# Mixer projections in three fp32r products, with the weights split on ScalarE, VectorE and GpSimd

## The chip, the core and the metric

The kernel runs on one core of one Trainium2 chip, as one program. The metric is the device time of that core in microseconds (us), from the start of the execution to its end. A profile of one execution, taken by the hardware profiler, stands beside the times; its span is the time between its first and its last recorded instruction.

## What is computed

The input `x` is 256 tokens of 1024 numbers in fp32. Four layers follow one another, each of a mixer and a feed-forward part. Cut to what matters:

```python
# first_block: two layers, with a norm behind each part as well
for layer in range(2):
    h = rmsnorm(x, norm_mix_pre[layer])
    m = attention_mixer(h, ...) if layer % 2 == 0 else recurrent_mixer(h, ...)
    x = x + rmsnorm(m, norm_mix_post[layer])
    h = rmsnorm(x, norm_ffn_pre[layer])
    x = x + rmsnorm(swiglu(h, ffn_w_gate[layer], ffn_w_up[layer], ffn_w_down[layer]), norm_ffn_post[layer])
# second_block: two layers
x = x + dilated_diff_mixer(rms_norm(x, attn_norm), ...)
x = x + swiglu_2(rms_norm(x, ffn_norm), ...)
x = x + hgrn2_mixer(rms_norm(x, hgrn_norm), ...)
x = x + moe_swiglu(rms_norm(x, moe_norm), ...)        # 8 experts, top 2, 3584 hidden units

def recurrent_mixer(h, w_in, ...):
    gate, xr = jnp.split(h @ w_in, 2, axis=-1)        # w_in: 1024 x 2048
    gate = jax.nn.gelu(gate, approximate=True)
    xc = causal_conv(xr, conv_w) + conv_b             # four taps
    r = sigmoid(xc @ w_a + b_a); i = sigmoid(xc @ w_i + b_i)   # in four blocks of 256
    ...                                               # a, sqrt(1 - a*a), a scan over the tokens: hs
    return (hs * gate) @ w_out
```

Each mixer begins with `h @ w_in`: its projection. The widths of the four `w_in` are 3072 (attention), 2048 (recurrent), 3072 (dilated and differential attention) and 4096 (HGRN2). These products are what the change rewrites.

## The kernel before, in words

**Stages.** The program has eight stages, in the order of the reference: `A` (attention mixer), `F` 0, `R` (recurrent mixer), `F` 1, `E` (dilated and differential attention), `F` 2, `G` (HGRN2) and `M` (the experts, in a loop over the eight of them). Below, first mixer means `A`, second `R`, third `E`, fourth `G`. Each stage has a function for each engine (`R_tensor`, `R_scalar`, `R_vector`); the order of its statements is the order of the instructions on that engine, and semaphores tie the engines together. Nothing reorders them: an instruction that waits holds up everything behind it on its engine.

**Weights.** SyncE loads all weights in units of 1 MB (128 partitions x 2048 fp32) in one fixed order into a ring of slots, five in the first seven stages and seven in `M`. A slot has the unit as loaded (`slot_raw`) and room for two fp32r parts of it: `slot_hi`, a rounded copy, and `slot_lo`, what the copy leaves over (the weights minus the high part). In the trace these are `ring`, and `ring_r` with the half 1 and 0 in its number. A slot is free for the next load when TensorE has counted `w_used` for its unit.

**Two kinds of product.** The feed-forward parts and the experts split each unit: ScalarE copies it (`highs_to`, a helper that does so for all units up to a given one that are not done yet; it waits for `landed`), VectorE subtracts (`lows_to`), and TensorE makes three fp32r products for each pair: high x high, high weight x low feature, low weight x high feature. The mixers' projections do not: `project` makes their units with `columns_of(w, c0, False)`, `weights_ready` waits for the load alone, and `by_columns` and `by_tokens` do one plain fp32 matmul on `slot_raw` and on the features in fp32 (`HTf`). A unit of a mixer is 256 columns of `w_in` over all 1024 features; by columns ("F" and "X" units) it makes 2 x 8 matmuls of 256 moving columns (the tokens), by tokens ("H" units) as many of 256 moving columns (the weights). The out projections (`project_out`) are plain fp32 in both kernels, and so are the gates of `R` (L1208).

**First units.** `first_tokens` runs the first three or four units of a mixer for tokens 0 to 127 first, in matmuls of 128 columns for "F" and "X" units, then for tokens 128 to 255. `unit_tensor` runs a later unit, `unit_scalar` evacuates it (L576) from PSUM (`ps`) with the function that the stage wants.

**Norms.** Between two stages each token half goes through sums of squares on ScalarE (`post_sums`, `norm_sums`), a small power on GpSimd (`norm_gpsimd`, which counts `s_rstd`), the gain on VectorE (`normalise_tokens`, L422), eight transposes on TensorE (`norm_turn`, L441) and evacuation of these. In front of a feed-forward part the evacuation gives a high part by ScalarE (`norm_high`, L368) and a low part by VectorE (`norm_low`, L433); in front of a mixer (`k % 2 == 0`) ScalarE and VectorE each copy half of it in fp32. There are two orders written out by hand: `norm_scalar` and `norm_vector` for mixers, `ffn_norm_scalar` and `ffn_norm_vector` for feed-forward parts, where copies and low parts of the first weights are interleaved.

**The second mixer's order.** TensorE: units 0 to 3 (the branch with the convolution), the gates of the first half, unit 4, the gates of the second half, units 5, 6, 7, out projection. ScalarE: convolution inputs, sigmoids of gates (L1250), tanh, exp (L1257), square roots (L1261), and only then the evacuations of units 4 to 7 with gelu (L576).

**The third and fourth mixer.** In `E` VectorE has a chain of reciprocals and gains (L1533, L1535) for the normalised queries and keys, and behind it the bias additions to the scores (L1546); ScalarE's squares (L1453) precede it. In `G` L576 evacuates the first units, and functions on ScalarE and VectorE follow before TensorE transposes (L1639).

**Entry to `M`.** ScalarE copies three units (`split_high`, L1953), then does the sums of both token halves; VectorE does the three low parts (`split_low`, L1958), then residual, gain and evacuation of both halves (L413, L422, L2146), then the arithmetic of the router (L2174 is a line of it). An expert gathers its tokens by fp32r matmuls of 128 columns (L1972).

**GpSimd** does the small powers, constants at the start (L795, L796) and issues the loads of the gain rows (`gpre`, `gpost`).

## Time and profile before

| | before |
|---|---|
| three executions, median (lowest to highest) | 2214.52 us (2212.74 to 2216.56) |
| profiled execution, its own time | 2214.71 us |
| span of the profiled execution | 2212.6 us |
| mean granted TensorE clock | 0.989 |
| TensorE busy | 2152.9 us, 10426 matmuls |
| VectorE busy | 1412.0 us |
| ScalarE busy | 1182.0 us |
| GpSimd busy | 42.6 us |

The page names engines PE (TensorE), DVE (VectorE), ACT (ScalarE), POOL (GpSimd) and SP (SyncE). `L509` is line 509 of the kernel; `ps<-arena,ring` names what is written and what is read. Views of the trace are: the page's busy shares; groups of instructions by line, where with shapes apart a group is one line, engine, operation and tile; the chain of work that ended last, followed back from the last instruction and shown in order of time; and the timeline of one engine. Matmuls are pipelined, and one that starts before the previous one ends overlaps it in the records, so that starts of successive matmuls tell what one costs. Idle time in square brackets stands ahead of an instruction with what released it.

### The profile page before, as it was taken

What the parts mean: (1) busy time and instruction counts of PE and PEld (TensorE: products, weight loads), DVE (VectorE), ACT (ScalarE), POOL (GpSimd) and SP (SyncE); (2) the same over time, 40 slices, a digit from 0 to 9 for tenths busy, and PEclk for the clock granted to TensorE, in tenths of its full rate; (3) what the DMA queues carried; (4) which work ended last, traced back from release to release, by engine and by line L of the source; (5) the groups of instructions that cost most, each with busy time, mean ns of one, the idle gap of its engine ahead of it and who ended that gap; (6) DMA issues with size and microseconds to landing.
All of it is one profiled execution on the core that took longest, in us unless ns stands there. A gap on an engine that the chain in (4) does not pass through costs nothing.

```text
span 2212.6 us, 26593 instructions
## 1 busy us (share of the span) xinstructions
PE 2152.9 (97%) x10426; PEld 1755.4 (79%) x10426; DVE 1412.0 (64%) x1193; ACT 1182.0 (53%) x1107; POOL 42.6 (2%) x94
## 2 busy tenths in 40 slices
PE   7999999999999999999996999999999999999998
PEld 7757889868888658889874888888888888888887
DVE  1425444454444635443725888889888988888887
ACT  1335432444423544333533677677766777767775
POOL 1001000010000000000000000000000000000000
PEclk9999999999999999999996999999999999999999
DMA  7325554555554226555423999999999999999997
GB/s 250 115 77 187 191 184 149 183 174 189 189 172 143 96 86 209 184 178 162 134 77 115 359 354 351 376 341 363 348 358 349 362 348 356 372 338 373 342 362 262
DMA packets 208180, 539.60 MB, mean 244 GB/s; under 512 B 10046, under 2 KB 67487, under 8 KB 208111
## 3 DMA queue, kind: packets, MB, share of 16 engines
q1 hardware_dynamic: 204224, 530.61, 67.7%
q0 software_dynamic: 2096, 7.87, 1.0%
q8 instruction: 51, 0.84, 0.2%
q10 hardware_dynamic: 1790, 0.14, 0.1%
q14 instruction: 19, 0.15, 0.0%
HBM read 537.54 MB, written 1.05 MB: 243 GB/s over the span
## 4 chain that ended last, share of the span: by engine, by line
PE 89%; ACT 5%; DVE 2%; issue 2%; DMA 1%; POOL 1%; DVEq 0%; ACTq 0%; POOLq 0%
PE ps L1962 12%; PE ps L1964 12%; PE ps L1963 12%; PE ps L509 12%; PE ps L622 5%; PE ps L623 5%; PE ps L624 5%; PE ps L586 4%; PE ps L527 4%; ACT ring_r L1953 3%; PE ps L663 3%; PE ps L665 3%; PE ps L664 3%; PE ps L1972 2%; PE ps L2017 1%
## 5 line engine op out<-in xcount | busy, mean ns | idle before, releaser
L1958 DVE TENSOR_TENSOR ring_r<-ring,ring_r 128x2048 fp32r<-128x2048 f32 x339 | 761.9, 2287 | 114.8 <-ACT ring_r L1953 114.7
L1953 ACT ACTIVATE ring_r<-ring 128x2048 fp32r<-128x2048 f32 x339 | 631.0, 1911 | 70.1 <-DMA ring<-in_moe_w_gate 60.1
L1962 PE MATMUL ps<-ring_r,arena_r 128*128 128x512 f32 x1344 | 532.0, 396 | 1.0 <-DVE arena_r L2200 1.0
L1964 PE MATMUL ps<-ring_r,arena_r 128*128 128x512 f32 x1344 | 524.6, 390 | 0.0
L1963 PE MATMUL ps<-ring_r,arena_r 128*128 128x512 f32 x1344 | 524.4, 390 | 0.0
L324 DVE TENSOR_TENSOR ring_r<-ring,ring_r 128x2048 fp32r<-128x2048 f32 x99 | 226.9, 2292 | 233.2 <-ACT ring_r L315 233.2
L1964 PEld LDWEIGHTS ps<-ring_r,arena_r 128*128 128x128 f32 x1344 | 252.7, 188 | 54.7
L1962 PEld LDWEIGHTS ps<-ring_r,arena_r 128*128 128x128 f32 x1344 | 253.0, 188 | 51.6 <-issue 1.2
L1963 PEld LDWEIGHTS ps<-ring_r,arena_r 128*128 128x128 f32 x1344 | 253.3, 188 | 50.5
L315 ACT ACTIVATE ring_r<-ring 128x2048 fp32r<-128x2048 f32 x99 | 189.3, 1915 | 181.3 <-DMA ring<-in_ffn_w_up 81.6
L509 PE MATMUL ps<-arena,ring 128*128 128x128 f32 (+1 forms) x1600 | 261.7, 324 | 3.6 <-ACT arena L368 2.7
L509 PEld LDWEIGHTS ps<-arena,ring 128*128 128x128 f32 x1600 | 235.5, 193 | 27.8 <-issue 7.6
L622 PE MATMUL ps<-ring_r,arena_r 128*128 128x512 f32 (+1 forms) x576 | 216.9, 377 | 2.3 <-DVE arena_r L433 1.4
L623 PE MATMUL ps<-ring_r,arena_r 128*128 128x512 f32 (+1 forms) x576 | 214.5, 372 | 0.0
L624 PE MATMUL ps<-ring_r,arena_r 128*128 128x512 f32 (+1 forms) x576 | 214.4, 372 | 0.0
L622 PEld LDWEIGHTS ps<-ring_r,arena_r 128*128 128x128 f32 x576 | 108.9, 189 | 22.5 <-DVE ring_r L324 2.0
L624 PEld LDWEIGHTS ps<-ring_r,arena_r 128*128 128x128 f32 x576 | 108.8, 189 | 19.0
L623 PEld LDWEIGHTS ps<-ring_r,arena_r 128*128 128x128 f32 x576 | 108.9, 189 | 18.8 <-issue 0.5
L2105 ACT ACTIVATE arena_r<-ps 128x512 fp32r<-128x512 f32 x56 | 33.5, 598 | 161.9 <-PE ps L2017 161.9
L586 PE MATMUL ps<-ring,arena 128*128 128x512 f32 x256 | 115.0, 605 | 2.1 <-ACT arena L1051 1.7
L663 PE MATMUL ps<-ring_r,arena_r 128*128 128x512 f32 x264 | 103.7, 393 | 0.0
L665 PE MATMUL ps<-ring_r,arena_r 128*128 128x512 f32 x264 | 102.9, 390 | 0.0
(322 smaller groups left out, 1798.4 us busy)
## 6 DMA issues: line engine op xcount, KB each, us to landing
ring<-in_moe_w_gate SPq DMA_DIRECT2D x115, 1024.0 KB, 5.3
ring<-in_moe_w_up SPq DMA_DIRECT2D x112, 1024.0 KB, 5.3
ring<-in_moe_w_down SPq DMA_DIRECT2D x112, 1024.0 KB, 5.0
ring<-in_ffn_w_gate SPq DMA_DIRECT2D x33, 1024.0 KB, 5.1
ring<-in_ffn_w_up SPq DMA_DIRECT2D x33, 1024.0 KB, 5.1
ring<-in_ffn_w_down SPq DMA_DIRECT2D x33, 1024.0 KB, 4.9
...
```

The source lines that it names most:

```text
L315: nc.scalar.activation(slot_hi(u), slot_raw(u), ACT.Copy).then_inc(w_hi, 1)
L324: nc.vector.tensor_tensor(slot_lo(u), slot_raw(u), slot_hi(u), ALU.subtract).then_inc(w_lo, 1)
L509: mm = nc.tensor.matmul(o, w[:, kt, f * P:f * P + P], HTf[:, ts, kt, :], start=(kt == 0), stop=(kt == KT - 1))
L586: mm = nc.tensor.matmul(Y[:, t, c * 512:(c + 1) * 512], x[:, 2 * r + kt, t * P:(t + 1) * P], w[:, kt, c * 512:(c + 1) * 512], start=(n == ...
L622: nc.tensor.matmul(o, HTh[:, t, k, :], wh[:, kt, :], start=(k == 0), stop=False)
L623: nc.tensor.matmul(o, HTl[:, t, k, :], wh[:, kt, :], start=False, stop=False)
L624: mm = nc.tensor.matmul(o, HTh[:, t, k, :], wl[:, kt, :], start=False, stop=(k == KT - 1))
L1953: nc.scalar.activation(unit_parts(k)[0], ring[:, slot_of(k), 0:2048], ACT.Copy).then_inc(m_hi, 1)
L1958: nc.vector.tensor_tensor(low, ring[:, slot_of(k), 0:2048], high, ALU.subtract).then_inc(m_lo, 1)
L1962: nc.tensor.matmul(out_, x[:, 0, f, :], w[0], start=first, stop=False)
L1963: nc.tensor.matmul(out_, x[:, 1, f, :], w[0], start=False, stop=False)
L1964: return nc.tensor.matmul(out_, x[:, 0, f, :], w[1], start=False, stop=last)
```

## The change

1. `project` makes split units, so the mixers' projections are three fp32r products like the feed-forward parts. The branches for plain fp32 in `by_columns`, `by_tokens`, `norm_high` and `norm_low` go; features are always a high and a low part.
2. High parts are ScalarE copies. Each stage calls `highs_to` for the first five units before its own work; from then on `unit_scalar` copies unit j + 3 after it has evacuated unit j (never beyond the plan's last), and `R_scalar` does so after each convolution input.
3. Low parts of the first four units of each mixer stay with VectorE. Those of `plan[4:]` go to GpSimd (`lows_gpsimd`), in four quarters of 512 columns, after the norm's powers of that stage; TensorE waits for `w_lo_pool`.
4. One order of the norm for all stages replaces the two: two copies of weights ahead of the first half's sums, the low parts between the steps of `norm_vector`. The end of a feed-forward part already splits the next unit.
5. The first token half's features are released in halves: `first_tokens` and the feed-forward code wait for the first 512 features, and for the second 512 only at their first use (`second`).
6. The first gain row is loaded through ScalarE's queue; the loads of the bias and of `gpost` come after the first norm's power on GpSimd. Two scratch places move (`A_sc[3]` to `dist`, `E_sc[2]` to page 9), since the features' high and low parts take the place.
7. At the entry to `M` the three splits are interleaved with the norm; in the router's arithmetic the weights' softmax, the fp32r identity and two memsets come after the selection of tokens (the functions between are moved as they are, and are not shown in the diff).

```diff
-                plan.append((kind, columns_of(w, c0, False), None if kind == "X" else evacs[0]))
+                plan.append((kind, columns_of(w, c0, True), None if kind == "X" else evacs[0]))
...
+        pool_units = [u for plan in (A_plan, R_plan, E_plan, G_plan) for _, u, _ in plan[4:]]
+        dve_units = [u for u in range(N1) if split_no[u] is not None and u not in pool_units]
+        low_at = {u: (w_lo, n + 1) for n, u in enumerate(dve_units)}
+        low_at.update({u: (w_lo_pool, 4 * n + 4) for n, u in enumerate(pool_units)})
...
-                if split_no[u] is not None:
+                if u in dve_units:
                     dve.wait_ge(w_hi, split_no[u] + 1)
                     nc.vector.tensor_tensor(slot_lo(u), slot_raw(u), slot_hi(u), ALU.subtract).then_inc(w_lo, 1)
+        def lows_gpsimd(pool, plan):
+            for _, u, _ in plan[4:]:
+                pool.wait_ge(w_hi, split_no[u] + 1)
+                for q in range(4):
+                    c = slice(512 * q, 512 * q + 512)
+                    nc.gpsimd.tensor_tensor(slot_lo(u)[:, c], slot_raw(u)[:, c], slot_hi(u)[:, c],
+                                            ALU.subtract).then_inc(w_lo_pool, 1)
         def weights_ready(pe, u):
             if split_no[u] is None:
                 pe.wait_ge(landed[u % NS_EARLY], landed_at(u))
             else:
-                pe.wait_ge(w_lo, split_no[u] + 1)
+                pe.wait_ge(*low_at[u])
...
-        def ffn_norm_scalar(act, k, first):
+        def norm_scalar(act, k, first):
             if has_post(k):
                 post_sums(act, k, 0)
+            if k:
+                highs_to(act, first + 1)
             norm_sums(act, k, 0)
+            highs_to(act, first)
             norm_high(act, k, 0)
-            highs_to(act, first + 2)
             if has_post(k):
                 post_sums(act, k, 1)
-                highs_to(act, first + 3)
-                norm_sums(act, k, 1)
-            else:
-                norm_sums(act, k, 1)
-                highs_to(act, first + 3)
+            highs_to(act, first + 2)
+            norm_sums(act, k, 1)
+            highs_to(act, first + 3)
             norm_high(act, k, 1)
-        def ffn_norm_vector(dve, k, first):
+        def norm_vector(dve, k, first):
             if has_post(k):
                 post_gain(dve, k, 0)
-            residual(dve, k, 0)
+            if k:
+                residual(dve, k, 0)
+                lows_to(dve, first + 1)
             normalise_tokens(dve, k, 0)
+            lows_to(dve, first)
             norm_low(dve, k, 0)
-            lows_to(dve, first + 1)
             if has_post(k):
                 post_gain(dve, k, 1)
-                lows_to(dve, first + 2)
+            lows_to(dve, first + 1)
+            if k:
                 residual(dve, k, 1)
-                lows_to(dve, first + 3)
-                normalise_tokens(dve, k, 1)
-            else:
-                residual(dve, k, 1)
-                lows_to(dve, first + 2)
-                normalise_tokens(dve, k, 1)
-                lows_to(dve, first + 3)
+            lows_to(dve, first + 2)
+            normalise_tokens(dve, k, 1)
+            lows_to(dve, first + 3)
             norm_low(dve, k, 1)
...
                 for kt in range(KT):
+                    if second and f == fs[0] and kt == KT // 2:
+                        pe.wait_ge(*second)
                     nc.tensor.matmul(o, wh[:, kt, c], HTh[:, ts, kt, :], start=(kt == 0), stop=False)
                     nc.tensor.matmul(o, wh[:, kt, c], HTl[:, ts, kt, :], start=False, stop=False)
                     mm = nc.tensor.matmul(o, wl[:, kt, c], HTh[:, ts, kt, :], start=False, stop=(kt == KT - 1))
...
         def first_tokens(pe, k, pairs):
-            if k % 2 == 0:
-                pe.wait_ge(s_hth, 4 * k + 2)
-            pe.wait_ge(s_htl, 4 * k + 2)
             for n, (u, bank, how) in enumerate(pairs):
                 if n == len(pairs) - 1:
                     norm_turn(pe, k, 1)
                 weights_ready(pe, u)
-                how(pe, u, bank, ts=(0,))
-            if k % 2 == 0:
-                pe.wait_ge(s_hth, 4 * k + 4)
-            pe.wait_ge(s_htl, 4 * k + 4)
-            for u, bank, how in pairs:
-                how(pe, u, bank, ts=(1,)).then_inc(w_used, 1)
+                if n == 0:
+                    pe.wait_ge(s_htl, 4 * k + 1)
+                how(pe, u, bank, ts=(0,), second=None if n else (s_htl, 4 * k + 2))
+            for n, (u, bank, how) in enumerate(pairs):
+                if n == 0:
+                    pe.wait_ge(s_htl, 4 * k + 3)
+                how(pe, u, bank, ts=(1,), second=None if n else (s_htl, 4 * k + 4)).then_inc(w_used, 1)
...
             nc.scalar.activation(dst, src, func, scale=scale).then_inc(s_evac, 1)
+            highs_to(act, min(plan[j][1] + 3, plan[-1][1]))
...
         def R_scalar(act, step):
-            norm_scalar(act, 2)
+            norm_scalar(act, 2, R_plan[0][1])
+            highs_to(act, R_plan[4][1])
...
                 ins.then_inc(r_x, 1)
+                highs_to(act, R_plan[0][1] + j + 3)
...
         def M_scalar(act, step):
-            for k in range(AHEAD):
-                split_high(act, 0, k)
+            split_high(act, 0, 0)
             norm_sums(act, 7, 0)
+            split_high(act, 0, 1)
             norm_sums(act, 7, 1)
+            split_high(act, 0, 2)
             for t in range(TT):
...
         def M_vector(dve, step):
-            for k in range(AHEAD):
-                split_low(dve, 0, k)
+            split_low(dve, 0, 0)
             for t in range(TT):
                 residual(dve, 7, t)
+                if t:
+                    split_low(dve, 0, 1)
                 normalise_tokens(dve, 7, t)
...
-            pool.dma_start(gpre[:, :], row_of(*norm_gains[0])).then_inc(gpre_in, 16)
+            norm_gpsimd(pool, step, 0, 0)
             pool.dma_start(A_bias, bass.AP(tensor=bias.tensor, offset=1,
                                            ap=[[1, P], [2 * REL_CLIP + 1, N_HEADS_A], [1, KEYS]])).then_inc(side_in, 16)
             pool.dma_start(gpost[:, :], row_of(*post_gains[0])).then_inc(gpost_in, 16)
-            norm_gpsimd(pool, step, 0, 0)
             norm_gpsimd(pool, step, 0, 1)
             setup_gpsimd(pool, step)
+            lows_gpsimd(pool, A_plan)
...
                 if k == 2:
+                    lows_gpsimd(pool, R_plan)
                     distances_gpsimd(pool, step)
+                elif k == 4:
+                    lows_gpsimd(pool, E_plan)
+                elif k == 6:
+                    lows_gpsimd(pool, G_plan)
...
+            act.dma_start(gpre[:, :], a[norm_gains[0][0]][norm_gains[0][1]].partition_broadcast(P)).then_inc(gpre_first_in, 16)
```

ScalarE in the second mixer, from the exp functions to the end of the stage, before. `r_tau`, `w_used` and `landed` are semaphores; `ring_r_1_..` is a slot's high part:

```order
L1257 ACT_TABLE_LOAD
L1257 ACTIVATE ring<-arena,small 128x256 x8
L1261 ACT_TABLE_LOAD
L1261 ACTIVATE ring<-ring 128x1024 [waits r_tau] x2
L576 ACT_TABLE_LOAD
L576 ACTIVATE ring<-ps 128x512 [waits w_used] x4
L315 ACTIVATE ring_r_1_56<-ring 128x2048 [waits landed3]
```

The same place now (L553 is the evacuation, L321 the copy of weights):

```order
L1244 ACT_TABLE_LOAD
L1244 ACTIVATE ring<-arena,small 128x256 x8
L1248 ACT_TABLE_LOAD
L1248 ACTIVATE ring<-ring 128x1024 [waits r_tau] x2
L553 ACT_TABLE_LOAD
L553 ACTIVATE ring<-ps 128x512 [waits w_used]
L321 ACTIVATE ring_r_1_52<-ring 128x2048 [waits landed1]
L553 ACTIVATE ring<-ps 128x512 [waits w_used]
L321 ACTIVATE ring_r_1_54<-ring 128x2048 [waits landed2]
L321 ACTIVATE ring_r_1_56<-ring 128x2048 [waits landed3]
L553 ACTIVATE ring<-ps 128x512 [waits w_used] x2
```

The copy of unit 5 stands behind the evacuation of unit 4, that of unit 6 behind the evacuation of unit 5.

TensorE in the second mixer, where the last gate matmuls meet unit 5, before:

```order
L1208 MATMUL ps<-arena,ring 128x256 [waits r_sig,r_xc]
L1208 MATMUL ps<-arena,ring 128x256 x3
L1208 MATMUL ps<-arena,ring 128x256 [waits r_sig]
L1208 MATMUL ps<-arena,ring 128x256 x3
L509 MATMUL ps<-arena,ring 128x256 [waits landed1]
L509 MATMUL ps<-arena,ring 128x256 x15
L509 MATMUL ps<-arena,ring 128x256 [waits landed2]
```

And now (L500 to L502 are the three products):

```order
L1193 MATMUL ps<-arena,ring 128x256 [waits r_sig]
L1193 MATMUL ps<-arena,ring 128x256 x3
L500 MATMUL ps<-arena_r_65,ring_r_1_52 128x256 [waits w_lo_pool]
L501 MATMUL ps<-arena_r_64,ring_r_1_52 128x256
L502 MATMUL ps<-arena_r_65,ring_r_0_51 128x256
```

A wait for a load has become a wait for GpSimd's low part.

VectorE at the entry to `M`, before. `m_hi` is counted by ScalarE's copies, `s_y` by TensorE's last out projection:

```order
L1958 TENSOR_TENSOR ring_r_0_49<-ring,ring_r_1_50 128x2048 [waits m_hi]
L1958 TENSOR_TENSOR ring_r_0_51<-ring,ring_r_1_52 128x2048 [waits m_hi]
L1958 TENSOR_TENSOR ring_r_0_53<-ring,ring_r_1_54 128x2048 [waits m_hi]
L413 TENSOR_TENSOR arena<-arena,ps 128x1024 [waits s_y]
L422 SCALAR_TENSOR_TENSOR arena<-arena,rstd,gpre 128x512 [waits s_rstd,gpre_in]
L422 SCALAR_TENSOR_TENSOR arena<-arena,rstd,gpre 128x512
```

And now:

```order
L1947 TENSOR_TENSOR ring_r_0_49<-ring,ring_r_1_50 128x2048 [waits m_hi]
L422 TENSOR_TENSOR arena<-arena,ps 128x1024 [waits s_y]
L434 SCALAR_TENSOR_TENSOR arena<-arena,rstd,gpre 128x512 [waits s_rstd,gpre_in]
L434 SCALAR_TENSOR_TENSOR arena<-arena,rstd,gpre 128x512
L2137 COPY arena<-ps 128x4x128 [waits s_tr] x2
L422 TENSOR_TENSOR arena<-arena,ps 128x1024 [waits w_used]
L1947 TENSOR_TENSOR ring_r_0_51<-ring,ring_r_1_52 128x2048 [waits m_hi]
```

One low part is left ahead of the first half's residual (L413 before, L422 now); the second stands behind the second half's.

## Rows read from the trace of the kernel before

**Rows 1.** The page's busy time, share of the span and instructions:
```profile
PE 2152.9 (97%) x10426; PEld 1755.4 (79%) x10426; DVE 1412.0 (64%) x1193; ACT 1182.0 (53%) x1107; POOL 42.6 (2%) x94
```
**Rows 2.** Groups by line, shapes apart: out<-in, count | busy, mean ns | idle before:
```profile
L509 PE MATMUL ps<-arena,ring 128*128 128x256 f32 x704 | 157.7, 381 | 0.0
...
L509 PE MATMUL ps<-arena,ring 128*128 128x128 f32 x896 | 104.4, 279 | 3.6 <-ACT arena L368 2.7 <-issue 0.9
...
L527 PE MATMUL ps<-ring,arena 128*128 128x256 f32 x384 | 87.9, 383 | 0.0
```
**Rows 3.** The chain in order of time: start, length, engine, line, count:
```profile
365.19 7.38 PE ps L509 x64
...
689.17 3.45 PE ps L509 x16
...
1316.01 2.63 PE ps L1972 x24
```
**Rows 4.** TensorE's timeline in the first feed-forward part: start, length, operation:
```profile
317.63 0.39 PE L622 MATMUL ps<-ring_r,arena_r 128*128 128x512 f32 x1
...
323.07 0.39 PE L663 MATMUL ps<-ring_r,arena_r 128*128 128x512 f32 x1
...
328.51 0.28 PE L622 MATMUL ps<-ring_r,arena_r 128*128 128x256 f32 x1
...
332.94 0.28 PE L623 MATMUL ps<-ring_r,arena_r 128*128 128x256 f32 x1
```
**Rows 5.** The page's costliest groups: the two halves of a split:
```profile
L324 DVE TENSOR_TENSOR ring_r<-ring,ring_r 128x2048 fp32r<-128x2048 f32 x99 | 226.9, 2292 | 233.2 <-ACT ring_r L315 233.2
...
L315 ACT ACTIVATE ring_r<-ring 128x2048 fp32r<-128x2048 f32 x99 | 189.3, 1915 | 181.3 <-DMA ring<-in_ffn_w_up 81.6
```
**Rows 6.** GpSimd's timeline at the start:
```profile
17.82 0.52 POOL L795 MEMSET scores_T<- 128x512 f32 x1
...
18.41 0.50 POOL L796 CAST iota_j<-distm 128x384 f32<-128x384 int32 x1
```
**Rows 7.** ScalarE's timeline, second mixer, behind the last gate matmul:
```profile
415.41 0.47 ACT L1250 ACTIVATE arena<-ps,cols 128x256 f32<-128x256 f32 x1 [0.89 <-PE ps L1208]
...
427.22 1.08 ACT L576 ACTIVATE ring<-ps 128x512 f32<-128x512 f32 x2
```
**Rows 8.** TensorE's timeline, second mixer (units 5 to 7) and fourth mixer:
```profile
415.21 20.88 PE L509 MATMUL ps<-arena,ring 128*128 128x256 f32 x96
...
1074.43 0.38 PE L1639 MATMUL ps<-ident,ring 128*128 128x128 f32 x2
```
**Rows 9.** VectorE's timeline in the third mixer:
```profile
690.00 3.35 DVE L1533 RECIPROCAL ring<-ring 128x512 f32<-128x512 f32 x1 [22.09 <-ACT ring L1453]
...
742.07 0.75 DVE L1535 SCALAR_TENSOR_TENSOR arena<-arena,cols,ring 128x512 f32<-128x512 f32 x1
...
749.17 1.13 DVE L1546 SCALAR_TENSOR_TENSOR ring<-dist,ps 128x384 f32<-128x384 f32 x2 [6.36 <-PE ps L1364]
```
**Rows 10.** ScalarE's timeline, fourth mixer, the last of the first evacuations:
```profile
1036.64 0.60 ACT L576 ACTIVATE arena<-ps 128x512 f32<-128x512 f32 x1 [2.98 <-PE ps L509]
```
**Rows 11.** TensorE's timeline: at the start, and transposes with idle time ahead:
```profile
14.59 13.59 PE L509 MATMUL ps<-arena,ring 128*128 128x128 f32 x96 [0.90 <-issue]
...
183.52 1.78 PE L441 MATMUL ps<-ident,arena 128*128 128x128 f32 x8 [2.95 <-DVE arena L422]
...
475.25 1.32 PE L441 MATMUL ps<-ident,arena 128*128 128x128 f32 x8 [2.62 <-DVE arena L422]
...
1177.48 1.97 PE L441 MATMUL ps<-ident,arena 128*128 128x128 f32 x8 [10.13 <-DVE arena L422]
```
**Rows 12.** ScalarE's timeline at the entry to the experts:
```profile
1165.73 1.91 ACT L1953 ACTIVATE ring_r<-ring 128x2048 fp32r<-128x2048 f32 x1 [15.21 <-DMA ring<-in_moe_w_gate]
```
**Rows 13.** VectorE's timeline in the router:
```profile
1198.95 0.16 DVE L2174 TENSOR_SCALAR rt<-rt 128x2 f32<-128x2 f32 x1
```
**Rows 14.** VectorE's timeline at the start of the program:
```profile
10.86 1.41 DVE L422 SCALAR_TENSOR_TENSOR arena<-arena,rstd,gpre 128x512 f32<-128x512 f32 x2 [8.80 <-DMA gpre<-in_norm_mix_pre]
```

108 lines of the change are left out of this document (44 added, 64 removed).

## The prediction

> **What bounds the kernel now.** I read the page's busy shares first: TensorE is busy for 97% of the span, ScalarE for about half, GpSimd for 2% [rows 1]. So the span is TensorE's own work plus its idle time, and the question is what a matmul costs back to back. The mean duration of a matmul doesn't tell that, because matmuls overlap; the chain of work and the timeline do. In the groups by line each projection matmul in plain fp32 is recorded twice, so the 704 + 384 records of 256 columns are 544 matmuls and the 896 records of 128 columns are 448 [rows 2]. The narrow ones are the first 3 or 4 column units of each mixer, which run token half by token half.
>
> From the chain: 16 records of 256 columns take 3.45 us, so one fp32 matmul of 256 columns takes 0.431 us; 64 records of 128 columns take 7.38 us, so a narrow one takes 0.231; 24 fp32r matmuls of 128 columns (the gather of the expert stage) take 2.63, or 0.110 each [rows 3]. From the timeline: between two starts with 24 fp32r matmuls of 512 columns 5.44 us pass, 0.227 each, and with 37 of 256 columns 4.43 us, 0.120 each [rows 4].
>
> **The matmuls themselves.** A product becomes three in fp32r. At 256 columns 3 x 0.120 = 0.360 against 0.431: 544 x -0.0715 = **-38.9 us**. At 128 columns 3 x 0.110 = 0.330 against 0.231: 448 x +0.099 = **+44.4 us**. So the arithmetic brings nothing: +5.5 us. What is gained on wide matmuls is lost on narrow ones, since an fp32r matmul of 128 columns is hardly cheaper than one of 256.
>
> **The splits.** Each of 48 units now needs ScalarE for 1.91 us, and then VectorE for 2.29 us (the first four of a mixer) [rows 5] or GpSimd for four quarters. The trace has no GpSimd operation of this kind with two inputs. A write alone of 512 elements takes 0.52 us, a cast of 384 elements with one input 0.50 [rows 6]. The bounds of a quarter are 0.52 (the write hides both reads) and 2 x 512 x 0.50 / 384 = 1.33 us (each input at the cast's rate); I take 1.2, near the upper end, because two inputs are read: 4.8 us for a unit, with both ends in the range. The Trainium skill, GPSIMD Engine Reference, section Performance versus the Vector engine, gives 4497 ns for a two-input operation of 2048 elements; by that the unit would be 4.5, within my bounds. Throughput is enough: 1.91 and 4.8 us are both under the 5.8 us that TensorE will need for a unit. What matters is when ScalarE reaches the copy in its program order.
>
> **The second mixer (recurrent), +31 us.** In ScalarE's order the copy of unit 5 of this plan stands behind the evacuation of unit 4, and that stands behind sigmoids, tanh, exp and square roots, which wait for TensorE's last gate matmuls. Before, this hurt nobody: TensorE had units 5 to 7 ready and ran them in 20.9 us beside those functions [rows 8]. ScalarE needs 12.4 us from the last gate matmul (its next sigmoid starts at 415.41) to the end of the first evacuation (427.22 plus half of 1.08) [rows 7]. Now, counted from that last gate matmul: copy of unit 5 done at 12.4 + 1.9 = 14.3, its low part at 19.2. TensorE is idle until then. It restarts slowly after such a gap: at the program's start the first projections, 96 records from 14.59 on, took 13.59 us where 48 x 0.231 = 11.1 would do [rows 11], so 2.5 lost; I take 2.2. Unit 5 ends at 27.2. Only then can ScalarE evacuate it (0.6) and copy unit 6 (1.9), GpSimd is done at 34.6, TensorE with unit 6 at 42.6 (slow again after 7 us of idleness) and with unit 7, whose parts are ready by then, at 48.4. Without waits it would be 20.7 - 3.4 = 17.3. That is **+31 us**, of it 27 idle. With a GpSimd quarter at 0.52 it would be 26, at 1.33 it would be 32.
>
> **The other mixers, +22 us.** The saving on wide matmuls counts only where TensorE is what is waited for. In the third mixer VectorE's chain of reciprocals runs from 690.00 to 742.8 with hardly a gap, and the scores behind it are used at 749.17 [rows 9], so of 9.2 us (8 units x 16 x 0.0715) little more than 1 can be had; ScalarE's copies push that chain back by 1.9 before it starts. I count 8 lost. In the fourth, from ScalarE's last first-unit evacuation at 1036.64 [rows 10] to the first transpose of the scores at 1074.43 [rows 8] ScalarE and VectorE have a chain of 35 us in hand while TensorE does 5.5 units; those now take 31.7 instead of 37.9, so the chain becomes the bound, with some 2 us of copies in it; later VectorE paces the loop over heads. I count 12 lost. In the first, the weights of the first heads wait behind one more copy: 2 lost. Bounds: 8 (only the chains, copies in gaps) and 35 (the whole saving, and copies on the path).
>
> **Edges of the stages.** At entry to a mixer VectorE has a low part of 2.29 us to do that stands ahead of the norm's operations: +1 each at three entries, **+3** (bounds 0 and 2.3 each). At entry to a feed-forward block the second half's sums come before the later copies and the first 512 features are released alone. Idle times of 2.95 and 2.62 us ahead of the transposes [rows 11] go, those run at full speed again (1.3), and about 2 come from the earlier release: **-9** (bound 0: the next split is late instead). Into the expert stage, the norm's first half waited behind three splits: ScalarE was idle for 15.21 us until a weight load landed [rows 12] and TensorE for 10.13 behind that [rows 11]. Now only one split, landed early, stands ahead. Idleness goes, and the 8 transposes take 0.9 rather than 1.97: -11.2; the gate operations at 1198.95, some six of 0.16 us [rows 13], move behind the selection: -1. Together **-12**; next to be late there is the second half's norm, which stays. At the start the gain row, for which VectorE waited 8.80 us [rows 14], comes by another queue 3 us earlier, but the first unit must land and be split: **-1**. Everything else in the expert loop is as it was, and it ends on TensorE.
>
> Sum: 5.5 + 31 + 22 + 3 - 9 - 12 - 1 = 39.5. The profiled execution took 2214.7 us (span 2212.6), the median is 2214.5. Forecast: **2254 us**.
>
> **Rivals.**
> *The cover holds elsewhere.* If the copies fall into ScalarE's gaps and VectorE's chains have slack that I don't see, the 22 us go and only the second mixer stalls: 2232. For it: ScalarE is half idle [rows 1]. Against: the chain of rows 9. Chance 0.20.
> *VectorE and GpSimd hold each other up.* No stage of this trace has both busy, so no row excludes it. Of the 32 GpSimd units 20 lie in the third and fourth mixers, 80 quarters; if one in three makes VectorE wait half a quarter, or is itself held, and the chain is VectorE's, that is 80 x 1/3 x 0.6 = 16 us, with 2 in the second mixer 18: 2272. The Trainium skill, SBUF - State Buffer, section Who interferes with whom, speaks against the change here: a VectorE instruction with two SBUF inputs and a GpSimd instruction that reads SBUF exclude each other for a whole instruction. No row of before shows it. Chance 0.17.
> *Narrow fp32r matmuls stream, and the time falls.* From 512 to 256 columns the spacing falls by 0.107 us [rows 4]. If it went on so, 128 columns would take 0.066 and not 0.110, and the 1344 narrow matmuls 59 us less: 2195, faster than before. It decides from a spacing under 0.080 (1344 x 0.030 = 40 us). Against it stands the gather, which has just this shape and type and runs at 0.110 [rows 3]; for it, that its operands are other tiles. The Trainium skill, TensorE: Matmul & The Clock Gate, section Back-to-back issue gap, gives about 81 ns for a sustained 128-column matmul; that would be 39 us less, 2215, no change. The row of the gather disagrees with it. Chance of something like this 0.07, most of it faster.
> *The change doesn't do what it says in the second mixer.* If the low part of unit 5 were ready in time, 31 us go: 2223. The order rows of ScalarE speak against it. Chance 0.05.
>
> **How the numbers follow.** The forecast with its neighbourhood (2240 to 2265) has 0.45, the four rivals 0.49, the rest lies outside on both sides, 0.02 below. The range from 2226 to 2280 takes in the first two rivals, all bounds of a quarter and of the edges, and leaves out the cases under 2226. About 0.2% (4.4 us) is what a measurement of this kernel can tell from no change. Faster 0.08, same 0.04, slower 0.88.
>
> **What would show it.** Right: in the second mixer TensorE idle for 17 to 20 us ahead of unit 5, released by GpSimd, and for 6 to 8 ahead of unit 6; narrow matmuls at 0.110 spacing and wide at 0.120; GpSimd quarters of 1.0 to 1.3 us; no 10 us gap ahead of the last norm's first transposes; the expert loop as long as before. Wrong: spacings under 0.08 for narrow matmuls, no GpSimd wait in the second mixer, or VectorE operations of the third and fourth mixers that last visibly longer.

## The result: 6% slower, far outside the range

| | before | the changed kernel |
|---|---|---|
| median of four executions (lowest to highest) | 2214.23 us (2212.74 to 2216.56) | 2349.23 us (2347.17 to 2350.11) |
| profiled execution, own time (span) | 2214.71 (2212.6) us | 2349.24 (2347.5) us |

The ratio is 1.0607, with a 95% interval of 1.0589 to 1.0626: 135 us more, where 40 were forecast and 66 was the range's end. The page of the changed kernel begins so; the first line answers to [rows 1], the group line (count, busy time, mean ns, idle before) has no counterpart before:

```profile
PE 2233.4 (95%) x11418; PEld 1864.0 (79%) x11418; DVE 1498.6 (64%) x1217; ACT 1271.0 (54%) x1163; POOL 222.3 (9%) x221
...
L338 POOL TENSOR_TENSOR ring_r<-ring,ring_r 128x512 fp32r<-128x512 f32 x128 | 173.8, 1389 | 279.6 <-ACT ring_r L321 279.6
```

TensorE's share has hardly fallen. 80 of the 135 us are busy time of TensorE and 54 idle time, so most of the loss is slow matmuls, and the next thing to do is to cut the span into stages. The table does that from the timelines of TensorE: a stage runs from the start of its first norm's transposes to that of the next stage, so that idle time ahead of the transposes counts with the stage before. In brackets stands, for the mixers, how much of the stage the clock was at its low level (ahead of its first rise it is taken as low, see below).

| us | start | A | F0 | R | F1 | E | F2 | G | M |
|---|---|---|---|---|---|---|---|---|---|
| before | 11.8 | 156.2 (8) | 195.3 | 96.7 (0) | 193.5 | 160.6 (7) | 190.9 | 172.5 (7) | 1035.1 |
| changed | 9.3 | 209.8 (101) | 191.7 | 140.1 (31) | 195.3 | 183.2 (34) | 192.2 | 192.5 (24) | 1033.3 |
| difference | -2.5 | +53.6 | -3.6 | +43.4 | +1.8 | +22.6 | +1.3 | +20.0 | -1.8 |

The four mixers have it all. Now TensorE's timeline of the changed kernel in the first mixer (start, length, operation, idle time ahead), at the beginning of the narrow products (those of 128 columns), amid them, and where the wide ones begin:

```profile
14.43 0.45 PE L500 MATMUL ps<-arena_r,ring_r 128*128 128x128 f32 x1 [3.21 <-DVE arena_r L441]
...
59.60 0.41 PE L500 MATMUL ps<-arena_r,ring_r 128*128 128x128 f32 x1
59.81 0.41 PE L501 MATMUL ps<-arena_r,ring_r 128*128 128x128 f32 x1
60.03 0.41 PE L502 MATMUL ps<-arena_r,ring_r 128*128 128x128 f32 x1
...
98.65 0.58 PE L513 MATMUL ps<-ring_r,arena_r 128*128 128x256 f32 x1
```

Successive starts are 0.213 us apart, not 0.110 as the gather in [rows 3]: all 382 spacings of the first mixer's narrow products are so, and 92 of the third's. In the second mixer, the fourth and the rest of the third they are 0.112 apart. The table by windows (stretch, busy time and count of each engine, granted clock, share and rate of transfers) ties this to the clock:

```profile
60.00:90.00 30.00, 30.00 (x143) 30.00 (x142) 0.00 (x0) 3.20 (x4) 0.00 (x0) 1.00 0.24 76
...
750.00:768.00 18.00, 18.00 (x86) 18.00 (x86) 7.25 (x6) 5.02 (x6) 2.45 (x4) 0.50 0.01 2
...
413.00:440.00 27.00, 27.00 (x243) 27.00 (x243) 12.70 (x16) 9.72 (x13) 7.44 (x8) 1.00 0.20 58
```

### The profile page after: what moved, and what is told of

It reads as the page before. It is cut to its first block, busy times and chain, and to the rows that moved or that the text cites. A ratio compares the mean times of both kernels' runs of the same rounds, so it can differ in the third digit from the quotient of the medians.

```text
span 2347.5 us, 28769 instructions
## 1 busy us (share of the span) xinstructions
PE 2233.4 (95%) x11418; PEld 1864.0 (79%) x11418; DVE 1498.6 (64%) x1217; ACT 1271.0 (54%) x1163; POOL 222.3 (9%) x221
## 4 chain that ended last, share of the span: by engine, by line
PE 83%; ACT 7%; DVE 6%; issue 2%; POOL 1%; DMA 1%; DVEq 0%; ACTq 0%; POOLq 0%; SPq 0%
PE ps L1951 12%; PE ps L1953 11%; PE ps L1952 11%; PE ps L600 5%; PE ps L601 5%; PE ps L602 5%; PE ps L500 4%; PE ps L501 4%; PE ps L502 4%; PE ps L564 4%; ACT ring_r L1942 3%; PE ps L641 2%; PE ps L643 2%; PE ps L642 2%; PE ps L1961 1%
## 5 line engine op out<-in xcount | busy, mean ns | idle before, releaser
L1947 DVE TENSOR_TENSOR ring_r<-ring,ring_r 128x2048 fp32r<-128x2048 f32 x339 | 761.8, 2287 | 95.3 <-ACT ring_r L1942 95.3
L1942 ACT ACTIVATE ring_r<-ring 128x2048 fp32r<-128x2048 f32 x339 | 629.5, 1911 | 46.3 <-DMA ring<-in_moe_w_gate 38.0
L1951 PE MATMUL ps<-ring_r,arena_r 128*128 128x512 f32 x1344 | 531.8, 396 | 1.0 <-DVE arena_r L2179 1.0
L1953 PE MATMUL ps<-ring_r,arena_r 128*128 128x512 f32 x1344 | 524.7, 390 | 0.0
L1952 PE MATMUL ps<-ring_r,arena_r 128*128 128x512 f32 x1344 | 524.4, 390 | 0.0
L330 DVE TENSOR_TENSOR ring_r<-ring,ring_r 128x2048 fp32r<-128x2048 f32 x115 | 263.5, 2291 | 262.1 <-ACT ring_r L321 262.1
L321 ACT ACTIVATE ring_r<-ring 128x2048 fp32r<-128x2048 f32 x147 | 281.1, 1913 | 215.9 <-DMA ring<-in_ffn_w_gate 90.5
L1953 PEld LDWEIGHTS ps<-ring_r,arena_r 128*128 128x128 f32 x1344 | 252.8, 188 | 54.7
L1951 PEld LDWEIGHTS ps<-ring_r,arena_r 128*128 128x128 f32 x1344 | 253.0, 188 | 51.5 <-issue 1.2
L1952 PEld LDWEIGHTS ps<-ring_r,arena_r 128*128 128x128 f32 x1344 | 253.1, 188 | 50.5
L500 PE MATMUL ps<-arena_r,ring_r 128*128 128x128 f32 (+1 forms) x800 | 254.0, 317 | 35.2 <-POOL ring_r L338 29.3
L501 PE MATMUL ps<-arena_r,ring_r 128*128 128x128 f32 (+1 forms) x800 | 248.5, 311 | 0.0
L502 PE MATMUL ps<-arena_r,ring_r 128*128 128x128 f32 (+1 forms) x800 | 248.3, 310 | 0.0
L500 PEld LDWEIGHTS ps<-arena_r,ring_r 128*128 128x128 f32 x800 | 179.6, 225 | 41.9 <-POOL ring_r L338 30.2
L338 POOL TENSOR_TENSOR ring_r<-ring,ring_r 128x512 fp32r<-128x512 f32 x128 | 173.8, 1389 | 279.6 <-ACT ring_r L321 279.6
L501 PEld LDWEIGHTS ps<-arena_r,ring_r 128*128 128x128 f32 x800 | 179.8, 225 | 1.7 <-issue 1.7
L502 PEld LDWEIGHTS ps<-arena_r,ring_r 128*128 128x128 f32 x800 | 179.6, 224 | 0.0
L2095 ACT ACTIVATE arena_r<-ps 128x512 fp32r<-128x512 f32 x56 | 33.5, 598 | 176.3 <-PE ps L2006 176.3
L600 PEld LDWEIGHTS ps<-ring_r,arena_r 128*128 128x128 f32 x576 | 108.5, 188 | 23.8 <-DVE ring_r L330 4.0
```

Source lines behind the costliest of these rows:

```text
L321: nc.scalar.activation(slot_hi(u), slot_raw(u), ACT.Copy).then_inc(w_hi, 1)
L500: nc.tensor.matmul(o, wh[:, kt, c], HTh[:, ts, kt, :], start=(kt == 0), stop=False)
L501: nc.tensor.matmul(o, wh[:, kt, c], HTl[:, ts, kt, :], start=False, stop=False)
L502: mm = nc.tensor.matmul(o, wl[:, kt, c], HTh[:, ts, kt, :], start=False, stop=(kt == KT - 1))
L600: nc.tensor.matmul(o, HTh[:, t, k, :], wh[:, kt, :], start=(k == 0), stop=False)
L1942: nc.scalar.activation(unit_parts(k)[0], ring[:, slot_of(k), 0:2048], ACT.Copy).then_inc(m_hi, 1)
```

## The experiments

What the spacings are in the profiled execution of each kernel below that still has narrow products, counted in TensorE's timeline (high is 0.11, low 0.21 us):

| high / low | A | R | E | G |
|---|---|---|---|---|
| changed | 0 / 382 | 286 / 0 | 192 / 92 | 382 / 0 |
| e1 | 340 / 39 | 286 / 0 | 193 / 91 | 382 / 0 |
| e2 | 234 / 148 | 19 / 267 | 285 / 0 | 381 / 0 |
| e3 | 232 / 150 | 3 / 283 | 190 / 95 | 382 / 0 |
| e4 | 0 / 382 | 2 / 283 | 205 / 79 | 382 / 0 |
| e7 | 237 / 145 | 198 / 87 | 285 / 0 | 382 / 0 |
| e9 | 333 / 48 | 19 / 266 | 190 / 95 | 381 / 0 |

Many cells differ although the code of that stage is the same. But where the low clock ends amid narrow products, it ends always at one place. The narrow products run on both sides of the second half's eight transposes (`ident` and `arena`, no fp32r tiles) in the first two mixers, and eleven times these were reached at the low clock. Five times the clock rose 0.1 to 1.5 us after them (first mixer of e1, e2, e3 and e7, second of e7), six times it did not. Here is e2 in the first mixer:

```profile
45.07 1.93 PE L449 MATMUL ps<-ident,arena 128*128 128x128 f32 x8
...
47.54 0.37 PE L501 MATMUL ps<-arena_r,ring_r 128*128 128x128 f32 x1
47.75 0.27 PE L502 MATMUL ps<-arena_r,ring_r 128*128 128x128 f32 x1
47.86 0.28 PE L500 MATMUL ps<-arena_r,ring_r 128*128 128x128 f32 x1
```

The transposes end at 47.00, and from 47.75 on the spacing is 0.11 instead of 0.21. Elsewhere amid narrow products no profile shows a rise but that of e9, in the burst that is told below; where the clock was still low at their end, it rose 2 to 6 us after the start of the wide products behind them. So whole times of kernels with narrow products are poor evidence, and stages have to be compared with their clock beside them.

**e1, the clock brought up beforehand.**

```diff
+            pe.wait_ge(warm_ok, 1)
+            warm(10)
             pe.wait_ge(ident_ok, 1)
             norm_turn(pe, 0, 0)
+            warm(6)
```

(`warm(n)`: n plain fp32 matmuls of 256 columns on a constant tile into a bank that is overwritten later.)

> The changed kernel with 16 extra plain fp32 matmuls of 256 columns on a constant tile in TensorE's idle time at the start (10 ahead of the first transposes, 6 behind them); nothing else differs. Theory (clock): in the changed kernel the 384 narrow fp32r matmuls of the first mixer start 0.213 us apart because TensorE is at the low clock when they begin, and this stream doesn't bring the high clock. Begun at the high clock they keep it, as in the fourth mixer (0.112). Expect spacing 0.112 from the first unit on and 38 us less: 2311. Rival (place): narrow fp32r matmuls of the first mixer are slow for another reason, such as its operands or the transfers beside them: spacing stays 0.21 and the time 2349. Second rival: the clock is high at first and falls within the narrow stream, some 10 to 30 us less.

Measured: 2315.59 in the profiled execution and 2344.71 in the other. First mixer 175.6 against 209.8, 340 of its narrow spacings 0.112: the products of this mixer are not slow by themselves, and the forecast of 38 was right to 4 us in the stage (the clock fell for 10 us within the stream, behind a 2.7 us wait for a low part, and rose with the transposes). The second execution shows that the same program can have the clock differently; it has no profile, and where it lost its 29 us isn't known.

**e9, a burst in the middle.** The same as extra work, behind the first narrow unit:

```diff
                 how(pe, u, bank, ts=(0,), second=None if n else (s_htl, 4 * k + 2))
+                if k == n == 0:
+                    pe.wait_ge(warm_ok, 1)
+                    for _ in range(16):
+                        nc.tensor.matmul(ps[:, 3, 0:256], page(7)[:, 0:P], page(7)[:, 0:256], start=True, stop=True)
```

> The changed kernel with pure extra work: behind the first narrow unit of the first mixer TensorE does 16 plain fp32 matmuls of 256 columns on a constant tile (6.9 us at the high clock, up to 13.7 at the low one). Theory (narrow stream keeps a low clock low): the burst brings the high clock and the narrow products behind it, if they keep it, start 0.112 apart: 336 x 0.101 = 34 us saved for about 11 spent; the first mixer's stage in the profile is 185 to 190 instead of 210. Where the clock falls again within the stream, part of that is lost. Rival (the first mixer's products are slow by themselves): the stage is 7 to 14 us longer than 210.

TensorE's timeline around the burst (L531; a plain fp32 matmul is recorded twice):

```profile
15.43 0.41 PE L503 MATMUL ps<-arena_r,ring_r 128*128 128x128 f32 x1
15.64 0.41 PE L501 MATMUL ps<-arena_r,ring_r 128*128 128x128 f32 x1
...
24.61 9.01 PE L531 MATMUL ps<-arena 128*128 128x256 f32 x32
...
33.62 0.28 PE L503 MATMUL ps<-arena_r,ring_r 128*128 128x128 f32 x1
33.74 0.27 PE L501 MATMUL ps<-arena_r,ring_r 128*128 128x128 f32 x1
```

The same instructions start 0.21 us apart ahead of the burst and 0.11 behind it, and stay there. The stage took 181.5, 28 less than 209.8 though it had 9 us of useless work more. Yet the median is 2349.42, no change: in the profiled execution (2349.08) what the first mixer gained the second lost, whose narrow products were at the low clock this time (266 of 285, stage 168.7 against 140.1). Two more executions took as long and the fourth 2319.57; these three have no profile. The Trainium skill (TensorE: Matmul & The Clock Gate, section What's actually happening) says that the throttled state is the default and activity releases it. The burst agrees: the granted clock rose 3.8 us after its start. The stream ahead of it does not: in the changed kernel 84 us of back-to-back work on fp32r matmuls of 128 columns passed at the low clock. There the measurement decides.

**e5, no narrow products.**

```diff
-            for n, (u, bank, how) in enumerate(pairs):
-                ...
+            norm_turn(pe, k, 1)
+            pe.wait_ge(s_htl, 4 * k + 4)
+            for u, bank, how in pairs:
+                weights_ready(pe, u)
+                how(pe, u, bank).then_inc(w_used, 1)
```

> The changed kernel, but the first three or four units of each mixer wait for the features of both token halves and then run in products of 256 columns, like the later units: no fp32r matmul of 128 columns is left in the mixers. Theory (narrow stream): the narrow stream costs 0.33 us where a wide product of half as many instructions costs 0.36, and it leaves the clock low once it is low. Wide units cost 5.8 us instead of 10.8 (at the high clock) or 20.5 (at the low one), against a wait of 8 to 12 us for the second token half. First mixer: 82 us of narrow products become 23 and a wait of 8, 50 less; second and fourth 6 and 12 less; third, where the clock was low for 24 us, 16 less: 2265 in all, and all runs alike within 5 us. Rival (the stream isn't to blame): the clock stays low at the start all the same, since it is set by the idle time before; then the first mixer gains some 20 only and the time is about 2300, with runs that differ by 20 and more.

Measured: 2284.82 (2282.63 to 2285.33), 64 less, and all four executions within 3 us. Stages: A 166.8, R 137.4, E 172.1, G 182.5. It gains less than forecast (84): the stages give 43 where 50 was forecast, 3 where 6, 11 where 16, and 10 where 12. In the first mixer the second token half's transposes start 19 us after the first's, not 8 to 12 (TensorE idle for 16.8 us ahead of them); in the others it is 7.5 to 10.3 us (idle 9 in the second and third, 6.5 in the fourth), as taken. But each of these waits ends at the low clock, which the forecast left out. What tells for the theory is the steadiness of the time, and that the first rise comes at 37.1 us, 4.8 after the start of the wide products.

**e2, copies earlier in the second mixer.**

```diff
                     nc.scalar.activation(R_i[:, j, :], bank[:, SEQ:], ACT.Sigmoid, bias=column("b_i", j)).then_inc(r_sig, 1)
+                highs_to(act, R_plan[6 + h][1])
                 act.wait_ge(r_sig, 4 * h + 4)
```

> The changed kernel with ScalarE's copies of units 5 and 6 of the second mixer moved behind the first four gates' sigmoids, and that of unit 7 behind the last four, ahead of tanh. Theory (order): the 21.8 and 7.5 us in which TensorE waits for GpSimd are there because these copies stand behind gelu evacuations; both go, and with them the restart at the low clock: 29 + 6 = 35 less, 2314. Rival (GpSimd's rate): 5.6 us per unit and the convolution's vector work beside it hold the low parts back anyway: some 8 to 12 us of idle time stay ahead of unit 5 to 7, 2325 to 2335.

First the changed kernel at this place, in the timelines of ScalarE, GpSimd and TensorE:

```profile
483.43 0.60 ACT L553 ACTIVATE ring<-ps 128x512 f32<-128x512 f32 x1
483.92 1.90 ACT L321 ACTIVATE ring_r<-ring 128x2048 fp32r<-128x2048 f32 x1
```
```profile
485.90 7.39 POOL L338 TENSOR_TENSOR ring_r<-ring,ring_r 128x512 fp32r<-128x512 f32 x4 [53.55 <-ACT ring_r L321]
```
```profile
493.34 0.58 PE L500 MATMUL ps<-arena_r,ring_r 128*128 128x256 f32 x1 [21.78 <-POOL ring_r L338]
...
509.56 0.58 PE L500 MATMUL ps<-arena_r,ring_r 128*128 128x256 f32 x1 [7.49 <-POOL ring_r L338]
```

Evacuation, copy, four quarters, TensorE: one chain, and TensorE idle for 21.8 and 7.5 us. In e2 both waits are gone (the times were 2317.19 and 2311.72), but the stage is 142.8 because its narrow products ran low (267 x 0.101 = 27 us), and 4.7 us of idle time are new ahead of the out projection. That the whole time met the forecast of 2314 is luck: the first mixer took 183.8 and the third 173.4, 36 less together, because more of their narrow products ran at the high clock. A better comparison is e8 with e5, both without narrow products. The stage is 108.6 against 137.4, 28.8 less, but e8 has the edits of e4 too. From the last gate matmul to the start of the out projection it is 22.0 us instead of 50.6, and the out projection is 1.6 longer at the low clock: **27 us** for this edit. GpSimd's rate, the rival, held nothing back.

**e3, no low parts by GpSimd.**

```diff
-            for _, u, _ in plan[4:]:
+            for _, u, _ in ():
...
-                pe.wait_ge(*low_at[u])
+                pe.wait_ge(*(low_at[u] if u in dve_units else (w_hi, split_no[u] + 1)))
...
-                    mm = nc.tensor.matmul(o, wl[:, kt, c], HTh[:, ts, kt, :], ...)
+                    mm = nc.tensor.matmul(o, wl[:, kt, c], (HTh if u in dve_units else HTl)[:, ts, kt, :], ...)
```

(`wl` is the high part for these units, and `by_tokens` is changed alike.)

> The changed kernel without GpSimd's low parts: for units 4 and later of each mixer the third product uses the high part of the weights and the low part of the features (so that the output is not the reference's), TensorE waits for ScalarE's copy alone, GpSimd does nothing there; the number and shape of matmuls is the same. Theory (exclusion): VectorE instructions that take 0.35 to 0.41 us alone take 1.3 to 1.5 while GpSimd's quarters run, so the chains of the third and fourth mixer are 8 to 12 us longer each; with the waits of TensorE for GpSimd in the fourth (12 us) and twice 5.6 us in the second: about 35 less, 2314. Rival (copies alone): the chains are longer because ScalarE's copies stand in them; then only the second mixer gains, 11 us: 2338.

Times 2313.93 (profiled) and 2299.75. That the first is the 2314 of the forecast is luck again: first mixer 30 less and second 17 more, both by the clock of their narrow products; TensorE's waits in the second mixer fell by 12.5 us (14.3 and 2.5 in place of 21.8 and 7.5). The fourth mixer fell by 21.3 us to 171.2, its narrow products high in both kernels. The timelines show why. VectorE in the changed kernel, with GpSimd beside it, and then VectorE at the same place of e3:

```profile
1179.58 1.38 DVE L1792 TENSOR_SCALAR ring<-ring,small 128x256 f32<-128x256 f32 x1
1180.88 1.38 DVE L1793 TENSOR_SCALAR ring<-ring,small 128x256 f32<-128x256 f32 x1
```
```profile
1179.52 5.20 POOL L338 TENSOR_TENSOR ring_r<-ring,ring_r 128x512 fp32r<-128x512 f32 x4 [4.17 <-ACT ring_r L321]
```
```profile
1164.99 0.41 DVE L1792 TENSOR_SCALAR ring<-ring,small 128x256 f32<-128x256 f32 x1
1165.32 0.34 DVE L1793 TENSOR_SCALAR ring<-ring,small 128x256 f32<-128x256 f32 x1
```

While GpSimd's four quarters run (5.20 us), VectorE's operations start 1.30 us apart, one for each quarter, and take 1.38 instead of 0.34 to 0.41. The two engines take turns. Operations that read one tensor from PSUM, and reciprocals (3.35 us in both cases), don't change. The Trainium skill (SBUF - State Buffer, section Who interferes with whom) calls it an exclusive lock on a shared pair of ports; the trace agrees, down to `TENSOR_SCALAR` with a single tensor input, which the page lists among those that can take it. The third mixer didn't fall (182.4 against 183.2, nearly the same clock): its chain is of reciprocals.

How much of the 21.3 us is this exclusion? TensorE's first transposes of the scores tell, in the changed kernel and then in e3:

```profile
1218.68 0.44 PE L1627 MATMUL ps<-ident,ring 128*128 128x128 f32 x2 [2.62 <-DVE ring L1829]
```
```profile
1191.37 0.69 PE L1627 MATMUL ps<-ident,ring 128*128 128x128 f32 x2 [6.54 <-DVE ring L1829]
```

That is 97.0 us into the stage against 84.3, and in both it is VectorE that comes last. VectorE begins its chain 46.7 us into the stage in both, waits for ScalarE no longer in the changed kernel than in e3, and is busy for 40.3 us with the 51 instructions up to there instead of 24.3. So 12.7 us are the exclusion, and TensorE's 12.3 us of waits for GpSimd's low parts lie hidden under it. The 8.6 us behind the transposes are not divided: there the changed kernel's TensorE waits for VectorE again (1.4 and 3.5 us) and part of the time is at the low clock.

**e7, the fourth mixer's low parts by VectorE.**

```diff
-        ... for plan in (A_plan, R_plan, E_plan, G_plan) for _, u, _ in plan[4:]]
+        ... for plan in (A_plan, R_plan, E_plan) for _, u, _ in plan[4:]]
+                low(max(4, u + 3))          # in VectorE's first loop, and so on through its chain
```

> The changed kernel, with the low parts of units 4 to 15 of the fourth mixer by VectorE (2.3 us each, between the steps of its chain) instead of GpSimd's quarters. Theory (exclusion): VectorE loses about 1 us in each of some 20 operations to GpSimd in this stage and TensorE waits 12 us for GpSimd's low parts; VectorE's own 7 low parts ahead of the first scores cost it 16 us, of which 7 lie in its gaps. Together 8 to 12 less in this stage: 182, against 192.5. Rival (load): VectorE's chain is as long as before with 16 us of own work instead of the exclusion, no change in the stage within 3 us. In both cases the whole time also depends on how long the clock stays low in the narrow streams of the first three mixers; the stage is what tells.

Times 2307.21 and 2335.91; the stage 176.3 against 192.5, 16.2 less, more than forecast. TensorE still waits, but for VectorE, and less: 2.3 and 5.2 us at the two places where it waited 4.4 and 7.9 for GpSimd. Twelve low parts of 2.3 us on the busier engine cost less than the same work on an idle one beside it.

**e4, norms ahead of copies.**

```diff
-            if k:
-                highs_to(act, first + 1)
             norm_sums(act, k, 0)
-            highs_to(act, first)
+            highs_to(act, first + 1 if k else first)
```

(and the same on VectorE.)

> The changed kernel with the first token half's sums ahead of ScalarE's copies of the next weights, and VectorE's gain operations ahead of the low parts, in every norm but the first. Theory: the copies that now stand ahead of the sums are what makes TensorE idle for 1.2 to 4.4 us ahead of the transposes of each stage; 2 to 3 us less at each of six entries, 12 to 15 in all: 2335. Rival: the split is needed as early as the features, so the idle time moves behind the transposes and the time is the same within 4 us.

Its executions took 2366.92, 2366.72, 2321.42, 2321.49 and 2320.97: two groups 45 us apart. The profile is of the first, where the second mixer's narrow products ran low (282 x 0.101 = 28 us more than in the changed kernel); what the shorter group had otherwise isn't known. So the whole time says nothing of the edit, and what follows compares idle times and the feed-forward stages, which have no narrow fp32r products of a mixer: the idle times of 3.96 and 4.40 us ahead of the transposes of F1 and F2 are gone, F1 is 192.9 (195.3) and F2 190.5 (192.2), F0 0.5 longer; into the second and third mixer it is 1.24 to 0.43 ahead of the transposes, but 0.84 to 2.24 ahead of the first product; the fourth mixer is the same within 0.1. Together that is some 11 us, a little under the 12 to 15, all of it at entries to feed-forward parts. At an entry to a mixer the rival is right.

**e6, the entry to the experts alone, on the kernel before.** The change's hunks in `M_scalar` and `M_vector`, nothing else.

> The kernel before, with the change's code at the entry to the experts alone (splits interleaved with the norm, the softmax of the router's weights, the fp32r identity and two memsets behind the selection). Theory: the 10.1 us of idle time ahead of the first transposes fall to 3.4 as in the changed kernel, the router's chain is 1 to 2 us shorter: 2205, faster than before by 9. Rival: next to be late is the second or third split, which the expert loop then waits for, and the gain is under 4 us: 2211.

Measured: **2200.91 us** (2200.0 to 2203.25), ratio 0.9946 (0.9929 to 0.9962), 4 us better than forecast. The last of [rows 11] are the transposes of the first token half; here are both halves:

```profile
1165.72 1.04 PE L441 MATMUL ps<-ident,arena 128*128 128x128 f32 x8
...
1175.29 1.97 PE L441 MATMUL ps<-ident,arena 128*128 128x128 f32 x8 [3.41 <-DVE arena L422]
```

The 10.1 us ahead of the first half are gone altogether and its transposes take 1.04 instead of 1.97. The 3.4 us that the expectation speaks of stand ahead of the second half, where it was 2.6 before; those transposes take 1.97 as before. The fourth stage is 162.2 instead of 172.5, the last 1032.7 instead of 1035.1.

**e8, all mends together.** e1, e2, e4, e5 and e7 in one.

> All mends together: the changed kernel with wide first units, 16 extra matmuls at the start that bring the high clock, ScalarE's copies of units 5 to 7 of the second mixer ahead of the exp and square roots, the first half's sums ahead of the copies at each stage's entry, and the fourth mixer's low parts by VectorE. Theory: the terms add up: 2265 - 27 (second mixer) - 10 (fourth) - 5 (entries) - 3 (start) = 2220, still no gain over the kernel before, because what wide fp32r products save (39 us by arithmetic) is lost on VectorE's and ScalarE's chains and the wait for the second token half. Rival: with everything mended the saving on wide products shows after all, 2195 to 2205, faster than before.

Measured: 2231.76 (2230.88 to 2232.58), ratio 1.0081, 12 us over the forecast, which built on 2265 for e5 and not on the 2285 measured. The extra matmuls at the start bring nothing here: the clock rose at 7.6 us and was low again from 17.8 on, within the 14.9 us in which TensorE waits for the second half. Stages A 166.8, R 108.6, E 168.8, G 167.1; against the kernel before with the better entry (e6: 156.4, 96.7, 159.9, 162.2) every mixer is still 5 to 12 us longer. In no mixer does the saving on wide products outweigh the rest.

**e10 and e11, the parts that were worth keeping.** On e6, `ffn_norm_scalar` and `ffn_norm_vector` with the later half of the change's order and the first 512 features released alone:

```diff
             norm_sums(act, k, 0)
+            highs_to(act, first + 1)
             norm_high(act, k, 0)
-            highs_to(act, first + 2)
             if has_post(k):
                 post_sums(act, k, 1)
-                highs_to(act, first + 3)
-                norm_sums(act, k, 1)
-            ...
+            highs_to(act, first + 2)
+            norm_sums(act, k, 1)
+            highs_to(act, first + 3)
             norm_high(act, k, 1)
```

> The kernel before with the change's code at the entry to the experts, and at the entry to the feed-forward parts its later half: the second token half's sums ahead of the last two copies, and the first 512 features released alone; the first half's sums stay ahead of the copies. Projections stay plain fp32. Theory: 2201 less 3 (first feed-forward part, 195 to 192) less 0.5 in each of the two others: 2197. Rival: the splits come late by what the sums come early: 2201.

Measured: **2197.07 us** (2195.33 to 2197.52), ratio 0.9919 (0.9906 to 0.9933), 17 us faster than the kernel before, as forecast; F0 191.6 (195.3 before). With the extra matmuls at the start:

> The kernel of the run before this one, with 16 extra plain fp32 matmuls of 256 columns in TensorE's idle time at the start. Theory: the first projections there run at the low clock for some 3 us; at the high clock from the start they take 11.1 instead of 13.6 us: 2.5 less, 2194.5. Rival: the extra matmuls themselves reach into the time of the first projections, or the clock falls in between: no gain, 2197.

Measured: 2196.63 (2195.65 to 2197.86), no difference that counts. The first rise of the clock moved from 20.0 to 7.5 us and the first mixer's stage from 156.5 to 155.5, not by 2.5. Without extra matmuls the clock rose 6 us after the start of the plain fp32 projections (13.95 in e10).

## Why the prediction was wrong

The step that failed is the price of a narrow product: "3 x 0.110" was read from a gather that ran at the high clock and was applied to 448 units of work without asking at what clock these would run. At the high clock it holds (0.112 measured, and 0.120 for 256 columns, as taken). At the low one it is 0.213, and 474 of the changed kernel's narrow products ran there: 474 x 0.101 = 48 us. The prediction did think of slow restarts, but priced each at 2.2 to 2.5 us, by the first projections of the kernel before [rows 11]; those were plain fp32, and the clock rose 5.5 us after their start. That the new stream could run on at the low clock was in no row of before.

By its terms:

- **Matmuls.** 5.5 us as arithmetic at the high clock; the clock adds 48.
- **First mixer.** 12.7 - 9.2 + 2 + 0 = 5.5 forecast, 53.6 measured. With the clock up for most of the stream (e1) it is 19.4. Its eight wide units did gain: from the start of the first of them to the start of the out projection it is 77.9 us in e1 and 81.0 before, 3 of 9 us. Up to the first of them e1 is 21.6 us behind: 13 are the narrow surcharge, 4 the spacings that are still low, 2.7 the wait within the stream and 2.3 the later start of the first product, which waits for its features' low part; the last two the prediction had at nothing.
- **Second mixer.** 31 us for the stall, 9.5 - 5.7 for the matmuls and 1 for the entry make 36; measured 43.4. The mechanism was right in place, releaser and size: 21.8 + 7.5 idle against 27 forecast, 27 recovered by reordering. The restarts cost 4.8 (units 5 to 7 took 8.7 and 13.4 us where 17.3 would do) against 4.4 forecast. Most of what the idle time has over the forecast is GpSimd's low part of unit 5, 7.39 us and not 4.8. Of the 7.6 us over the forecast these two make some 3, and the idle time at the stage's end, told under the entries, makes 4.0.
- **GpSimd's quarter.** 1.2 forecast with an upper bound of 1.33. Alone it takes 1.25 (4.99 us for four at 1143.51), but the mean is 1.39 and the longest 2.79; the bounds didn't allow for a wait for VectorE.
- **Third mixer.** 9.5 - 10.3 + 8 + 1 = 8 forecast (the prediction's text counts 8 wide units here, its total goes with 9), 22.6 measured; 12.7 in e7, where the clock stayed up through the narrow products. The clock is 10 of the missing 14, the idle time at the stage's end (4.4) the rest.
- **Fourth mixer.** 12.7 - 13.7 + 12 + 1 - 10 (the idle time at its end that goes) = 2 forecast, 20.0 measured. The 12 "because the chain becomes the bound" were wrong: without GpSimd's low parts (e3) the stage is 171.2, 9 over e6's 162.2, which is less than the narrow surcharge of 14.4 that the timelines show (29.5 us from the first to the last narrow product before, 43.9 now; 12.7 forecast). So some 5 us of the wide products' saving of 13.7 came through there. The rest, 21 us, is the rival "VectorE and GpSimd hold each other up", priced at 16 for both later mixers and given 0.17. It came true in one of them alone: 12.7 of the 21 are VectorE's longer chain (e3), the other 8.6, behind the first transposes, are not divided.
- **Entries.** Experts -12 forecast, -13 measured between the medians (e6), and as forecast: no idle time ahead of the first transposes, and these at 1.04 us. Feed-forward -9 forecast; measured -3.6, +1.8 and +1.3 in the three stages, and +4.0 and +4.4 at the ends of the two mixers ahead of them, so +8. The forecast looked at the second half's sums, which were moved ahead of copies; the same hunk puts two copies ahead of the first half's, and TensorE waits for its first transposes instead of its second:

```profile
550.93 1.97 PE L449 MATMUL ps<-ident,arena 128*128 128x128 f32 x8 [3.96 <-DVE arena L434]
```

- **Start.** -1 forecast, -2.5 measured.

Of the rivals, "narrow fp32r matmuls stream, and the time falls" looked at the right quantity and erred in sign: the spacing was 0.112 and 0.213 us, never under 0.080. The range reached to 2280 because all its cases took the clock for granted; that was its fault, not its width.

Not settled: why the second mixer's narrow products meet the low clock in e2, e3, e4, e9 and in part e7 and not in the changed kernel or e1, with nearly the same instructions in that stage, and why the second half's transposes bring the clock up in five of eleven cases. Executions of one kernel fall into groups (e4), so it may be small shifts in time; nothing here shows it.
